# Gate units of a hybrid decoder trunk placed beside the dilated attention batches alone

## What is computed

```
h = rms_norm(x, attn_norm[i])
c_q, c_kv, k_r, q_d, k_d, v_d, g_mla, g_dil = jnp.split(h @ w_in[i], split_at, axis=-1)
...
o_mla = mla_attention(q_nope, q_rope, k_nope, k_rope, v_mla).reshape(B, S, -1)      # 8 heads
o_dil = dilated_mixer(q_d.reshape(shp), k_d.reshape(shp), v_d.reshape(shp)).reshape(B, S, -1)  # 3 groups of 8 heads
merged = (jax.nn.sigmoid(g_mla) * (o_mla @ w_br_mla[i])
          + jax.nn.sigmoid(g_dil) * (o_dil @ w_br_dil[i]))
x = x + merged @ w_out[i]
```

## Time and profile before

| | us |
|---|---|
| median of three runs | 2085.05 |
| lowest and highest run | 2083.92, 2088.79 |
| span of the profiled execution, first to last instruction | 2074.7 |
| TensorE busy (matmuls) | 1948.2 (94%) |
| VectorE busy | 1490.1 (72%) |
| ScalarE busy | 1233.9 (59%) |
| attention batches of layer 0, from pass 3 on to the last values | 174.8 to 286.0 |
| the same of layer 1 | 809.1 to 924.3 |

### The profile page before, as it was taken

One profiled execution on the slowest core, in us unless ns is written; L12 is line 12 of the kernel. 1 busy time (PEld: TensorE's weight loads), 2 busy tenths in 40 slices (PEclk: granted clock), 3 DMA queues, 4 the chain that ended last, 5 costly groups with the idle time before them and its releaser, 6 DMA issues.

```text
span 2074.7 us, 26735 instructions
## 1 busy us (share of the span) xinstructions
PE 1948.2 (94%) x9278; PEld 1630.1 (79%) x9278; DVE 1490.1 (72%) x1659; ACT 1233.9 (59%) x1533; POOL 77.0 (4%) x131
## 2 busy tenths in 40 slices
PE   6998998999977998998799999999999999999986
PEld 5887886788866887877688888888888888888874
DVE  5456545556645455545598999989999898999974
ACT  4545353444434545444377787777877777787873
POOL 3100001000001300001000000000000000000001
PEclk9999798999998999789699999999999999999998
DMA  7652134555534553114399999999999999999980
GB/s 261 208 168 82 41 103 146 172 182 188 193 127 133 185 171 114 41 61 162 98 368 361 344 371 340 358 342 353 367 340 359 350 359 362 341 370 339 353 317 31
DMA packets 248963, 496.01 MB, mean 239 GB/s; under 512 B 7824, under 2 KB 11408, under 8 KB 248896
## 3 DMA queue, kind: packets, MB, share of 16 engines
q1 hardware_dynamic: 247552, 490.76, 67.3%
q0 software_dynamic: 1344, 4.36, 0.7%
HBM read 494.05 MB, written 1.05 MB: 239 GB/s over the span
## 4 chain that ended last, share of the span: by engine, by line
PE 91%; DVE 4%; ACT 2%; issue 2%; DMA 1%; POOL 1%; DVEq 0%; ACTq 0%; SPq 0%; POOLq 0%
PE ps L1329 27%; PE ps L1330 26%; PE ps L1331 26%; DVE lo L921 2%; PE ps L1597 2%; PE ps L1462 2%; PE ps L1444 1%; PE ps L1605 1%; PE ps L1346 1%; PE ps L1410 1%; DMA raw<-in_w_in 1%; ACT hi L618 1%; PE ps L1455 1%; PE ps L1433 0%; ACT pT L721 0%
## 5 line engine op out<-in xcount | busy, mean ns | idle before, releaser
L921 DVE TENSOR_TENSOR lo<-raw,hi 128x1024 fp32r<-128x1024 f32 (+1 forms) x936 | 1105.5, 1221 | 246.8 <-ACT hi L618 246.1
L618 ACT ACTIVATE hi<-raw 128x1024 fp32r<-128x1024 f32 (+1 forms) x936 | 969.4, 1054 | 415.6 <-PE ps L1331 403.5
L1329 PE MATMUL ps<-hi,hs_hi 128*128 128x512 f32 x896 | 357.1, 399 | 8.8 <-DVE lo L921 8.8
L1329 PE MATMUL ps<-hi,hT_hi 128*128 128x512 f32 (+1 forms) x832 | 339.2, 408 | 15.9 <-DVE hT_lo L955 7.6
L1331 PE MATMUL ps<-hi,hs_lo 128*128 128x512 f32 x896 | 350.7, 391 | 0.0
L1330 PE MATMUL ps<-lo,hs_hi 128*128 128x512 f32 x896 | 350.1, 391 | 0.0
L1330 PE MATMUL ps<-lo,hT_hi 128*128 128x512 f32 (+1 forms) x832 | 331.8, 399 | 0.0
L1331 PE MATMUL ps<-hi,hT_lo 128*128 128x512 f32 (+1 forms) x832 | 330.7, 397 | 0.0
L1329 PEld LDWEIGHTS ps<-hi,hs_hi 128*128 128x128 f32 x896 | 169.0, 189 | 45.4 <-DVE lo L921 12.3
L1329 PEld LDWEIGHTS ps<-hi,hT_hi 128*128 128x128 f32 x832 | 163.8, 197 | 51.6 <-DVE hT_lo L955 7.5
L1331 PEld LDWEIGHTS ps<-hi,hs_lo 128*128 128x128 f32 x896 | 168.8, 188 | 36.4
(11 more groups left out here) (259 smaller groups left out, 1865.9 us busy)
## 6 DMA issues: line engine op xcount, KB each, us to landing
raw<-in_moe_w_gate SPq DMA_DIRECT2D x112, 1024.0 KB, 5.8
raw<-in_moe_w_up SPq DMA_DIRECT2D x112, 1024.0 KB, 6.1
raw<-in_moe_w_down SPq DMA_DIRECT2D x112, 1024.0 KB, 5.9
raw<-in_w_in SPq DMA_DIRECT2D x56, 1024.0 KB, 5.0
raw<-in_dense_w_gate SPq DMA_DIRECT2D x14, 1024.0 KB, 5.1
raw<-in_dense_w_up SPq DMA_DIRECT2D x14, 1024.0 KB, 5.1
raw<-in_dense_w_down SPq DMA_DIRECT2D x14, 1024.0 KB, 5.0
raw<-in_w_out SPq DMA_DIRECT2D x8, 1024.0 KB, 5.0
```

Source lines behind the costliest of these rows:

```text
L618: a.activation(dst, src, ACT.Copy).then_inc(hi_done, 1)
L921: v.tensor_tensor(dst, src, h, ALU.subtract).then_inc(lo_done, 1)
L1329: pe.matmul(o, ah, wh[:, kk, :], start=(first and kk == 0), stop=False)
```

## The change

The table of passes is another one. Every pass from 7 (the second dilated batch) to 19 has one unit, 0 to 12 in order. No MLA batch has one, and none of the passes 20 to 23. `gate_evac` comes in passes 10, 14 and 18, since those have units 3, 7 and 11; the special case for pass 6 goes. On ScalarE and VectorE the splits hang on the same table and move with it. Units 13, 14 and 15 stay where they were.

```diff
-GATE_AT = {n + 2: n for n in range(4)}
-GATE_AT.update({NB_M + 2 + 2 * k: 4 + k for k in range(8)})
-GATE_AT[NB + 1] = 12
+GATE_AT = {NB_M + 1 + n: n for n in range(13)}
...
-                    j = 3 if n == NB_M else GATE_AT.get(n, 0)
-                    if j % 4 == 3 and n >= NB_M:
+                    j = GATE_AT.get(n, 0)
+                    if j % 4 == 3:
                         done(b + U_G + j)
                         gate_evac(j // 4, ACT.Copy, y.ev_act)
                     if n in GATE_AT:
```

## The result

The changed kernel took 2099.93 us (median of four runs, 2098.43 to 2103.49), the kernel before 2084.53 beside it (2083.92 to 2088.79). The ratio is 1.0068, 95% interval 1.0046 to 1.0090: slower, as forecast, and 2 us from the forecast of 2098. The traced execution has a span of 2096.7 us, 22.0 over the one of before, although the medians are 15.4 apart.

What follows compares the result with a forecast made beforehand. Waits on a chain through three engines and a low granted clock bound the attention stretches. Layer 0: +5.2 - 3.3 + 1.6 + 5 = +8.5; layer 1: +2.5 - 4.6 + 1.6 + 5 = +4.5; together +13, 2098 us, range 2081 to 2109.

Steps and rivals of the forecast that it cites:

- Step 2 and the MLA steps: TensorE passes 2 to 7: -2.1 us from an earlier turn in pass 2, low clock after; +5.2 and +2.5 by layer.
- the other bound: TensorE passes 2 to 7 if the clock stays full: 20.6 - 2.1 us, so -3.5 and -6.2 by layer.
- Steps 8 to 19: Twelve TensorE passes, all with a gate unit: even ones 5.35 us, odd ones 5.9, together 67.5 at full clock.
- The stalls: Units 4, 8 and 12 wait for ScalarE's gate copies in passes 11, 15, 19: 1.9 us each, 5.6 a layer.
- The splits: Splits on ScalarE and VectorE, one on each per gated pass, 1.05 and 1.22 us: costed at nothing.
- The clock behind the stalls: After the waits in passes 11, 15, 19: low clock behind one in three, 1.7 us lost, +1.6 a layer.
- The end: Passes 20 to 23, last values and unit 13: 12.8 us without unit 13 at full clock; low clock adds +5, bounds 0 and 6.5.
- steps 21 (half): Low-clock cost in the ungated last passes: 0.5 us for half of pass 21, then pass 22, pass 23 and unit 13.
- The signs: Expected in the changed trace: passes 3 to 6 idle 1.0 to 1.6 us at clock 0.5; passes 8 to 19 about 73 us.
- the clock holds: Rival: full clock in the MLA passes and the end, -17.6 us, 2067 us; chance 12%.
- Low in the MLA steps alone: Rival: low clock only in the MLA passes, end and stalls full; -0.2 us, 2085 us; chance 20%.
- As ragged as today: Rival: clock in gated passes 8 to 19 as low as before, +10.8 us in place of 1.6 twice; 2116 us; chance 8%.

Runs made afterwards that it cites:

- after_warm: The changed kernel with filler matmuls, read by nobody, in its ungated passes 3 to 6 and 20 to 22; 2069.67 us, ratio 0.9926 to the kernel before.
- after_early: The changed kernel with ScalarE's copies of the gate banks moved ahead of the same pass's exponentials; 2084.03 us, ratio 0.9973 to the kernel before.
- mla_back: The changed kernel with units 0 to 3 put back beside MLA batches 2 to 5; 2087.02 us, ratio 0.9996 to the kernel before.
- end_covered: The changed kernel with units 11 and 12 moved from passes 18 and 19 to 22 and 23; 2088.18 us, ratio 1.0024 to the kernel before.

## Why the prediction was right, and where it was off

**Direction and mechanism** held: the clock is low in the MLA steps and in the end, and each handover stalls. The forecast was 2098 us, measured were 2099.93, but that the size came so close is in part luck, as the last point shows. By its own steps, in the two layers:

- *Step 2 and the MLA steps.* Forecast +5.2 and +2.5. From the first scores to the end of step 7 the traces give 37.8 - 33.6 = +4.2 and 38.6 - 34.6 = +4.0. The low clock was the right choice; `after_warm` shows the other bound, which was right to 0.6 us in layer 0. In layer 1 step 2 gave back 0.8 us and not 2.1: its turn came early, but the clock had fallen by then (0.70 over the step).
- *Steps 8 to 19.* 67.5 us forecast for the gated steps, 67.4 and 67.3 in `after_early`, where nothing disturbs them. The stalls were 1.86 each against 1.9. The splits cost nothing, as said.
- *The clock behind the stalls.* Forecast one in three and 1.6 us a layer. It fell behind one of three in layer 0 (1.6 us) and behind all three in layer 1 (5.7 us: steps of 9.05, 9.28 and 10.49 in place of 7.7). This term was mis-sized for layer 1, and one in three was too low a share: in `after_warm`, `mla_back` and `end_covered` 13 of 14 stalls were followed by a low clock. What decides it at a given stall, no run shows.
- *The end.* Forecast +5 for the clock, bound 6.5; measured 18.3 - 12.8 + 4.79 - 2.86 = +7.4 in layer 0 and +7.6 in layer 1, over the bound. What failed is "steps 21 (half)", with nothing for step 20. In layer 0 the clock was low for the turn of step 20 already: step 20 took 4.79 us and not 3.5, step 21 took 5.6 and not 3.97.
- *The signs.* The forecast's sign for the MLA steps, 1.0 to 1.6 us of idle time at a clock of 0.5, joined the waits of the full clock with the low one: steps 4 to 6 had 0.2 to 0.7. For steps 8 to 19 it named 73 us, though its own terms give 67.5 + 5.6 + 1.6 = 74.7; measured were 74.5 and 78.7. Outside the two stretches nothing moved, as forecast: from the first scores to the end of unit 13 the layers grew by 9.8 and 12.5 us, and the span by 22.0.
- *The sum.* The forecast's +13 (8.5 and 4.5 by layer) was made against a trace of 2074.7 us of span. The traces differ by 22.0, the medians by 15.4. Two errors met. The terms above were some 9 us too small, 8 of them in layer 1. And the trace they were set against lay some 8 us under the median of its kernel, since a run's time is its span and 1.7 us (2098.43 and 2096.7 for one execution; 2074.7 and 1.7 are 2076.4, near the lowest run of the kernel before on record, 2075.78). The prediction had taken the distance of about 10 us for what lies around the span. Against the second trace of the kernel before, of 2079.2 us, the span grew by 17.5. The 2 us between forecast and result are thus owed in part to two errors that cancel.

**The rivals.** That the clock holds (2067 us) is ruled out by the trace of the changed kernel, with clocks of 0.59 and 0.52 over the MLA steps. "Low in the MLA steps alone" too: the end was low in both layers. "As ragged as today" didn't come: 0.98 and 0.91 over steps 8 to 19, though layer 1 went half of the way (5.7 us of that rival's 10.8).

**The Trainium skill**, "TensorE: Matmul & The Clock Gate", section "Why this matters for your kernels", names long idle gaps between bursts as the reason of a mid-kernel drop. A long gap does end at the low clock here: behind the 10.6 us of idle time ahead of 661.9 us in the changed kernel's trace, the next 5.5 us ran at 0.50. But no long gap is needed. In the kernel before the clock fell beside bare steps of 4 us with 0.9 us of idle time, and in the changed kernel it stayed low through MLA steps 4 to 6 with waits of 0.7 us and less. The advice of that section to keep TensorE busy does agree: the fillers brought the clock to 1.00.

The place of the change is thus a trade. It takes a clock loss of 14 to 16 us a layer out of the dilated steps and pays with one as large in MLA and in the end (7.7 and 7.4 us in layer 0), and with three stalls a layer that a different order on ScalarE would have spared.

## What to carry to other kernels

Where a pipeline's steps are bound by waits and there are spare matmuls to hide, spread them in small pieces over all of its steps. What a step needs is enough work to cover its wait and to keep the clock, and here half a unit in each of two steps did more than a whole unit in one of them. Read the granted clock by step before placing anything, and price a bare step at half clock, with the steps next to it. Read more than one trace of the kernel before, and set the span of each beside the timed runs. When a producer closes up, look at who must free its buffer and what stands ahead of that in its queue.

## What the runs showed of the hardware that was not expected

Work that nobody reads can pay: 56 filler matmuls a layer took 28 us off. A busy TensorE can stay at half clock: over steps 3 to 7 of layer 1 in the changed kernel it was busy for 27.28 of 29.40 us, at a clock of 0.52. A stall of 1.86 us can cost twice its length, its own and as much again at the low clock: in `after_warm` there were 11.4 us of low clock behind six of them. And the kernel before has a spread of its own of nearly 20 us (2075.78 to 2095.53 over thirteen runs). Its two traces are 4.5 apart, and 3.9 of that lies where the clock fell in layer 0.
